# Gate and up products of the gated stages as one 512-column matmul per weight tile, halves added outside PSUM

## What is computed

```
def swiglu(h, w_in, w_out):
    a, b = jnp.split(h @ w_in, 2, axis=-1)
    ...
# hier_moe: all 32 experts are computed, cw is zero for those not chosen
hid = jax.nn.silu(jnp.einsum('td,edf->tef', xt, w_gate)) * jnp.einsum('td,edf->tef', xt, w_up)
y = jnp.einsum('tef,efd->td', hid * cw[:, :, None], w_down)
# second_block: one ada vector per layer, c_act @ ada_w, 9216 wide
mod = (c_act @ ada_w[i] + ada_b[i]).reshape(bsz, N_SUB, 3, d)
```

## Time and profile before

| | us |
|---|---|
| median of 3 runs (4406.71 to 4414.47) | 4406.94 |
| the profiled execution, its own time | 4407.91 |
| its span in the trace | 4406.1 |
| TensorE busy | 3966.8 (90%) |
| VectorE busy | 2775.8 (63%) |
| ScalarE busy | 1760.8 (40%) |
| GpSimd busy | 1453.6 (33%) |

### The profile page before, as it was taken

The page is one execution under the profiler, slowest core; times in us unless marked ns, Lnnn a source line. Parts: engine busy times, 40 slices in busy tenths (PEclk is TensorE's granted clock), DMA queues, the critical chain, the costliest instruction groups (busy, mean ns, idle before and its releaser), DMA issues.

```text
span 4406.1 us, 69783 instructions
## 1 busy us (share of the span) xinstructions
PE 3966.8 (90%) x29036; PEld 3589.8 (81%) x29036; DVE 2775.8 (63%) x5143; ACT 1760.8 (40%) x3006; POOL 1453.6 (33%) x804
## 2 busy tenths in 40 slices
PE   7998997979979899979898998989898989799889
PEld 6657996679979886769898967989868989767689
DVE  4446776567767666557776946777647643765542
ACT  3233443434435443224444633444344443432243
POOL 2003443034425432025443421535304444420144
PEclk9658998689989998979999978999869999879899
DMA  5103662146636520016575413757415744310143
GB/s 200 50 37 136 247 248 99 53 158 234 250 138 258 210 102 25 1 58 262 211 275 200 151 56 110 278 208 273 179 64 218 268 155 161 106 39 1 43 157 112
DMA packets 63690, 664.40 MB, mean 151 GB/s; under 512 B 7056, under 2 KB 7568, under 8 KB 7952
## 3 DMA queue, kind: packets, MB, share of 16 engines
q1 hardware_dynamic: 63376, 659.94, 39.8%
HBM read 658.86 MB, written 1.05 MB: 150 GB/s over the span
## 4 chain that ended last, share of the span: by engine, by line
PE 78%; DVE 16%; ACT 3%; issue 2%; POOL 0%; DMA 0%; SPq 0%; DVEq 0%; ACTq 0%
PE pb L269 75%; PE pb L276 3%; DVE wp L226 2%; DVE wk L238 2%; ACT wp L264 2%; DVE wk L226 2%; DVE sq L226 2%; DVE sq L238 1%; DVE hT L238 1%; DVE ada_acc L238 1%; ACT wk L264 1%; DVE xT L238 1%; DVE nt L226 1%; DVE hx L238 0%; DVE hT L232 0%
## 5 line engine op out<-in xcount | busy, mean ns | idle before, releaser
L269 PE MATMUL pb<-hx,wp 128*128 128x256 f32 x15744 | 2014.7, 289 | 91.8 <-DVE hx L226 54.3
L269 PEld LDWEIGHTS pb<-hx,wp 128*128 128x128 f32 x15744 | 1968.4, 196 | 118.4 <-issue 78.5
L226 POOL TENSOR_TENSOR wp<-ring,wp 128x1024 fp32r<-128x1024 f32 (+1 forms) x606 | 1286.9, 2141 | 2252.2 <-ACT wp L264 2252.2
L264 ACT ACTIVATE wp<-ring 128x1024 fp32r<-128x1024 f32 x936 | 940.5, 1046 | 328.2 <-PE pb L269 246.2
L226 DVE TENSOR_TENSOR wp<-ring,wp 128x1024 fp32r<-128x1024 f32 (+1 forms) x650 | 770.5, 1201 | 372.1 <-ACT wp L264 371.2
L269 PE MATMUL pb<-ex,wp 128*128 128x256 f32 x5856 | 754.9, 286 | 2.1 <-DVE ex L226 2.1
L269 PEld LDWEIGHTS pb<-ex,wp 128*128 128x128 f32 x5856 | 721.0, 193 | 23.1 <-issue 20.6
L238 DVE SCALAR_TENSOR_TENSOR ada_acc<-ring,cact,ada_acc 128x384 f32<-128x384 f32 x576 | 530.2, 984 | 58.1 <-ACT ada_acc L264 58.1
L269 PE MATMUL pb<-wk 128*128 128x128 f32 (+8 forms) x3136 | 497.2, 330 | 15.6 <-ACT wk L264 6.2
L269 PEld LDWEIGHTS pb<-wk 128*128 128x128 f32 (+4 forms) x3136 | 346.3, 193 | 162.2 <-issue 98.1
L226 DVE TENSOR_TENSOR sq<-sq,pb 128x256 f32<-128x256 f32 (+1 forms) x360 | 161.6, 449 | 351.7 <-ACT sq L264 304.4
(11 more groups left out here) (175 smaller groups left out, 3010.5 us busy)
## 6 DMA issues: line engine op xcount, KB each, us to landing
ring<-weights SPq DMA_DIRECT2D x385, 1536.0 KB, 6.6
ring<-weights SPq DMA_DIRECT2D x41, 1024.0 KB, 4.9
ring<-weights SPq DMA_DIRECT2D x4, 512.0 KB, 10.2
cst<-consts SPq DMA_DIRECT2D x1, 2032.0 KB, 11.8
ring<-weights SPq DMA_DIRECT2D x1, 1280.0 KB, 5.5
prm<-params SPq DMA_DIRECT2D x1, 1258.0 KB, 7.3
ring<-weights SPq DMA_DIRECT2D x1, 1152.0 KB, 4.9
xT<-xT_in SPq DMA_DIRECT2D x1, 1024.0 KB, 4.8
```

The source lines that it names most:

```text
L226: return self.real.tensor_tensor(out, a, b, op) if self.real else Uncounted()
L264: return self.real.activation(out, a, func, bias=bias, scale=scale, accum_out=accum)
L269: return self.real.matmul(out, l, r, start=start, stop=stop, skip_group_check=skip)
```

## The change

The input tile `hx` is laid out so that the high and the low half of a block lie side by side (512 columns). For each block the weight's high part is now multiplied with all 512 columns at once, high halves into columns 0 to 255 of the bank, low halves into 256 to 511; the weight's low part is multiplied with the high half, into columns 0 to 255, as before. Gate and up need a bank each. The two halves of a bank are added outside: ScalarE copies the upper one to SBUF (`sg`, or the new single buffer `su`), VectorE adds the lower one. In `moe`, the scale per token and the weight per expert are then applied apart to `sg` and `su`, and one multiplication joins them.

```diff
-    Hh, Hl = v3(hx, 0, 8, T), v3(hx, 2048, 8, T)
+    HX = v3(hx, 0, 8, 2 * T)
+    Hh, Hl = HX[:, :, 0:T], HX[:, :, T:2 * T]
...
+    su = sq[:, 512:768]
...
         def products(u):
-            key = (st, "glu", u)
-            ps = bk.take(e, key, (v_out, key))
-            for b, p in enumerate(g.pieces[u][0:2]):
+            for b, (name, p) in enumerate(zip(("gate", "up"), g.pieces[u][0:2])):
+                key = (st, name, u)
+                if u == g.first == 2:
+                    ps = bk.hold(e, b, key, (v_out, key))
+                else:
+                    ps = bk.take(e, key, (v_out, key))
                 split_ready(e, p)
                 for k in range(KD):
...
-                    ins = mm3(e, ps[:, b * T:(b + 1) * T], part((p.hi, p.lo), k * 128), in_hx(k), k == 0, k == KD - 1)
-                ins.then_inc(*product.up(("used", p.at), *([key] if b else [])))
+                    hi, lo = part((p.hi, p.lo), k * 128)
+                    e.mm(ps[:, :], hi, HX[:, k, :], k == 0, False, skip=True)
+                    ins = e.mm(ps[:, 0:T], lo, Hh[:, k, :], False, k == KD - 1, skip=True)
+                ins.then_inc(*product.up(("used", p.at), key))
...
@@ glu_act
         def hidden(u):
...
+            e.wait_ge(*product[st, "gate", u])
+            if u >= 3:
+                e.wait_ge(*x_lo[st, "hid", u - 3])
+            e.act(sg[n], bank(st, "gate", u)[:, T:2 * T], ACT.Copy).then_inc(*a_out.up((st, "gate", u)))
+            e.wait_ge(*product[st, "up", u])
+            if u:
+                e.wait_ge(*v_step[st, "both", u - 1])
+            e.act(su, bank(st, "up", u)[:, T:2 * T], ACT.Copy).then_inc(*a_out.up((st, "up", u)))
+            e.wait_ge(*(v_step[st, "gate", u] if cw else v_out[st, "gate", u]))
+            e.act(sg[n], sg[n], ACT.Silu).then_inc(*a_step.up((st, "silu", u)))
...
-            e.wait_ge(*v_out[st, "cw" if cw else "glu", u])
+            e.wait_ge(*v_step[st, "both", u])
             e.act(eh[n], sg[n], ACT.Copy).then_inc(*x_hi.up((st, "hid", u)))
...
@@ glu_dve
         def hidden(u):
...
+            e.wait_ge(*a_out[st, "gate", u])
+            e.tt(sg[n], sg[n], bank(st, "gate", u)[:, 0:T], ALU.add).then_inc(*v_out.up((st, "gate", u)))
+            e.wait_ge(*a_out[st, "up", u])
+            e.tt(su, su, bank(st, "up", u)[:, 0:T], ALU.add).then_inc(*v_out.up((st, "up", u)))
             if cw:
...
-                e.tt(sg[n], ps[:, 0:T], rsb[:, :], ALU.mult).then_inc(*v_step.up((st, "gate", u)))
...
-                e.tt(sg[n], sg[n], pcw[:, 0:T], ALU.mult).then_inc(*v_out.up((st, "cw", u)))
+                e.tt(sg[n], sg[n], rsb[:, :], ALU.mult).then_inc(*v_step.up((st, "gate", u)))
+                e.wait_ge(*v_out[st, "up", u])
                 e.wait_ge(*summed[st, "cw", u])
-            else:
-                e.wait_ge(*a_out[st, "silu", u])
-                e.tt(sg[n], sg[n], ps[:, T:2 * T], ALU.mult).then_inc(*v_out.up((st, "glu", u)))
+                e.tt(su, su, bank(st, "cw", u)[:, 0:T], ALU.mult).then_inc(*v_out.up((st, "cw", u)))
+            e.wait_ge(*a_step[st, "silu", u])
+            e.wait_ge(*(v_out[st, "cw", u] if cw else v_out[st, "up", u]))
+            e.tt(sg[n], sg[n], su, ALU.mult).then_inc(*v_step.up((st, "both", u)))
             e.wait_ge(*x_hi[st, "hid", u])
             e.tt(el[n], sg[n], eh[n], ALU.subtract).then_inc(*x_lo.up((st, "hid", u)))
```

More of the change, by code:

```diff
@@ L929, in hidden @@
             n = u % 3
-            ps = bank(st, "glu", u)
+            e.wait_ge(*a_out[st, "gate", u])
+            e.tt(sg[n], sg[n], bank(st, "gate", u)[:, 0:T], ALU.add).then_inc(*v_out.up((st, "gate", u)))
+            e.wait_ge(*a_out[st, "up", u])
+            e.tt(su, su, bank(st, "up", u)[:, 0:T], ALU.add).then_inc(*v_out.up((st, "up", u)))
             if cw:
-                pcw = bank(st, "cw", u)
-                e.wait_ge(*product[st, "glu", u])
                 e.wait_ge(*v_step[st, "rs"])
-                if u >= 3:
-                    e.wait_ge(*product[st, "down", u - 3, 7])
-                e.tt(sg[n], ps[:, 0:T], rsb[:, :], ALU.mult).then_inc(*v_step.up((st, "gate", u)))
-                e.wait_ge(*a_out[st, "silu", u])
-                e.tt(sg[n], sg[n], ps[:, T:2 * T], ALU.mult).then_inc(*v_out.up((st, "glu", u)))
-                e.wait_ge(*v_out[st, "glu", u])
+                e.wait_ge(*v_out[st, "gate", u])
+                e.tt(sg[n], sg[n], rsb[:, :], ALU.mult).then_inc(*v_step.up((st, "gate", u)))
+                e.wait_ge(*v_out[st, "up", u])
                 e.wait_ge(*summed[st, "cw", u])
-                e.tt(sg[n], sg[n], pcw[:, 0:T], ALU.mult).then_inc(*v_out.up((st, "cw", u)))
-            else:
-                e.wait_ge(*a_out[st, "silu", u])
-                e.tt(sg[n], sg[n], ps[:, T:2 * T], ALU.mult).then_inc(*v_out.up((st, "glu", u)))
+                e.tt(su, su, bank(st, "cw", u)[:, 0:T], ALU.mult).then_inc(*v_out.up((st, "cw", u)))
+            e.wait_ge(*a_step[st, "silu", u])
+            e.wait_ge(*(v_out[st, "cw", u] if cw else v_out[st, "up", u]))
+            e.tt(sg[n], sg[n], su, ALU.mult).then_inc(*v_step.up((st, "both", u)))
             e.wait_ge(*x_hi[st, "hid", u])
```

## The result

| | before | after |
|---|---|---|
| median of 6 executions, us | 4409.41 (4399.08 to 4414.47) | 4426.31 (4421.24 to 4427.84) |
| span of the profiled execution, us | 4406.1 | 4424.7 |
| TensorE / VectorE busy | 90% / 63% | 89% / 70% |

The account below looks back on a forecast made before the run. PE bounds the gated stages before; after the change DVE was to bound those with ada. Terms 34 (six ffn) + 15 (moe) - 12 (two ffn without ada) = +37 on 4406.1: 4443 us, range 4380 to 4490.

Parts of the forecast that it names:

- VectorE becomes the bound through the held multiply: ffn with ada: second unit's multiply, two SBUF inputs, waits for POOL's piece; DVE's pair 18.44 us, above PE's 17.40.
- The term of the six stages: Six ffn stages with ada: ten pairs at 18.44 us make each 5.6 us longer, +34 in all.
- Rival 2: ffn with ada: operations count, not ports; multiply not held, DVE pair 17.1 under PE's 17.4, time 4342; 15%.
- DVE in moe: moe stages: scale with two SBUF inputs held, DVE's pair 18.04 becomes 20.25 us; +7.5 each, +15.
- PE's saving of 17 ns a block: Gated products: wide plus narrow matmul take 343 ns per block in place of 360; 0.27 us a unit.
- The two stages without ada: Last two ffn stages: DVE has time free, PE gains 344 blocks x 17 ns; -5.8 each, -12.
- the sum: Whole kernel: 34 + 15 - 12 = +37 on the span of 4406.1, 4443 us.
- The term for all untouched stages: Stages outside the gated ones: no change entered in the sum, their time taken from the profile before.
- rival 4: PE's new waits bring the clock to 1.2 GHz, or ACT copies come late: 4560, or 4480 if only moe; 7%.

Follow-up runs that it names:

- psum_sum: Changed kernel, but the up sum (in moe also the gate sum) is written back to its PSUM bank: 4381.94 us, 0.9933 of before.
- last_two: New products, copies and additions only in stages 15 and 17, eight gated stages in the old form, hx in the new layout: 4404.5 us, ratio 0.9988.
- the filling: Eight matmuls added at TensorE's wait ahead of mamba's head loop: kernel before 4382.94 us, changed kernel 4426.90, psum_sum 4371.06.

## Why the prediction was wrong, and where it was right

- **VectorE becomes the bound through the held multiply: right.** 1.71 us seen, pair 18.40 against 18.44; psum_sum shows the cause. The term of the six stages, +34, measured +33.9. Rival 2's pair of 17.1 without a hold is what psum_sum brought about.
- **DVE in moe: right in kind, somewhat too large.** Pair 19.97 against 20.25. The first profile has +5.5 for each of the two stages' stretches against the +7.5 forecast; over four executions the whole is at +9.7 to +15.2.
- **PE's saving of 17 ns a block: mis-sized.** 7 ns. The two stages without ada gave -4.8, not -12. That the wide one's 223 came near the 227.5 measured is luck. The row behind it, 222 ns, is of matmuls on unsplit fp32 operands, which leave two records each (16 for eight matmuls), and it is not the longest pitch of the trace: two records of 256 columns at 2581.10 start (2582.01 - 2581.10) / 2 = 455 ns apart, at the 1.2 GHz level. The narrow one was charged at 120, its pitch among its like.
- **The step that failed is the sum.** It took all that the change does not touch at its time in the one profile of before, and the mamba stage there owed some 23 us (325.4 - 302.5) to the clock's lower level. The term for all untouched stages was 0 without a reason given, and measured -21.2. The gated terms, 33.9 + 10.7 - 4.8, are +39.8, 3 above my +37, since a moe term too large by 4 and a saving too large by 7 nearly cancel; mamba's -20.4, and -0.8 elsewhere, make the +18.6 of the profiles. I had asked of the clock only whether the new waits would bring it down (rival 4, which did not come: PEclk is 0.98 from 1330 to 1500), never where in the trace it was down already, and so what might come up. PEclk of 0.71 from 2600 to 2650, in mamba, stood in the trace before.
- **What stays open** is why the changed kernel's executions lie more often at the short mamba stage than those of the kernel before. Layout (last_two) did not do it, nor a shift of 12 or 29 us in the one execution of each, and the changed kernel itself was seen at 305, 317 and 324. The cause of the loss, the wait of 4.83 us ahead of the loop, is shown by the filling; what decides how long the clock then stays down is not.

## What to carry to other kernels

Before work is moved from TensorE to VectorE, find VectorE's shortest period in the late state and the operations in it with two SBUF inputs that meet a GpSimd piece: writing an intermediate sum back to PSUM took one such input away, and the addition still took 0.42 us. A difference of two medians can hold a change in the granted clock somewhere else that is larger than the change under study; compare stage by stage, and look at the clock in stages nobody touched. Where a wait of TensorE stands ahead of a loop that TensorE bounds, a few matmuls into a free bank may be a cheap gain: 26 us in the kernel before, and none to speak of in the changed one.

## What was unexpected of the hardware

TensorE stayed at the 1.2 GHz level for tens of microseconds while it was busy without a break: 40.00 of 40.00 us at 0.50 in one execution of the changed kernel, in a window that stood at 0.91 in another. Most of the matmuls there are thin (32 rows, or 64 columns of weights). With the clock brought down by a wait of 4.83 us ahead of this loop, being busy did not bring it back at once, and how long it took differed between executions of one program: 5, 33 and 47 us, with mamba at 305.0, 317.3 and 324.1 us.
